# Attention scores in fp32r from stacked high and low key parts, in the mixers of the last two blocks

## The reference, cut to what matters

```python
def _diff_attention(dq, dk, dv, lam):
    s = jnp.einsum('bqhjd,bkhjd->bhjqk', dq, dk).astype(jnp.float32) * ATTN_SCALE
    p = jax.nn.softmax(s, axis=-1)
    a = (p[:, :, 0] - lam * p[:, :, 1]).astype(dv.dtype)
    return jnp.einsum('bhqk,bkhe->bqhe', a, dv)

def _gqa_attention(gq, gk, gv):
    s = jnp.einsum('bqhgd,bkhd->bhgqk', gq, gk).astype(jnp.float32) * ATTN_SCALE
    p = jax.nn.softmax(s, axis=-1).astype(gv.dtype)
    return jnp.einsum('bhgqk,bkhd->bqhgd', p, gv)
```

## Time and profile before

| | us |
|---|---|
| median of 3 runs | 4083.15 (4079.98 to 4084.63) |
| the profiled execution, its own time | 4075.62 |
| its span, first to last instruction | 4073.8 |
| TensorE busy | 3853.2 (95%) |
| VectorE busy | 2133.5 (52%) |
| ScalarE busy | 1346.3 (33%) |
| GpSimd busy | 1484.0 (36%) |

### The profile page before, as it was taken

One profiled execution on the slowest core, in us unless ns is written; L12 is line 12 of the kernel. 1 busy time (PEld: TensorE's weight loads), 2 busy tenths in 40 slices (PEclk: granted clock), 3 DMA queues, 4 the chain that ended last, 5 costly groups with the idle time before them and its releaser, 6 DMA issues.

```text
span 4073.8 us, 48594 instructions
## 1 busy us (share of the span) xinstructions
PE 3853.2 (95%) x18340; PEld 3096.0 (76%) x18340; DVE 2133.5 (52%) x2959; ACT 1346.3 (33%) x1779; POOL 1484.0 (36%) x1012
## 2 busy tenths in 40 slices
PE   8999898999998989999999899999798999999999
PEld 7888775877886848757888778888675757777887
DVE  5555846036776361457732357777644348624334
ACT  3222644242224242352232332222424252334223
POOL 3555341436663202103433224444221305544443
PEclk9999999999999999999999999999899999999999
DMA  5554221224442101101122123333110202222222
GB/s 216 185 188 174 75 94 39 103 81 154 157 155 85 56 1 52 47 1 49 66 73 73 52 104 124 124 124 124 48 52 21 78 1 83 93 103 75 95 98 83
DMA packets 57650, 367.28 MB, mean 90 GB/s; under 512 B 5792, under 2 KB 12192, under 8 KB 14112
## 3 DMA queue, kind: packets, MB, share of 16 engines
q1 hardware_dynamic: 42064, 271.11, 19.1%
q10 hardware_dynamic: 15440, 94.12, 6.2%
HBM read 363.11 MB, written 2.10 MB: 90 GB/s over the span
## 4 chain that ended last, share of the span: by engine, by line
issue 62%; POOL 28%; PE 9%; POOLq 0%; DVE 0%; ACT 0%; DVEq 0%; ACTq 0%
POOL b_wlo L602 28%; PE ps L1768 3%; PE ps L1770 3%; PE ps L1769 3%; POOLq L616 0%; DVE b_y L1260 0%; POOLq L618 0%; DVE b_x L1264 0%; DVE b_y L1317 0%; PE ps L1844 0%; ACT b_whi L643 0%; PE ps L1831 0%; ACT b_xout L709 0%; DVE b_small L1262 0%; POOLq L602 0%
## 5 line engine op out<-in xcount | busy, mean ns | idle before, releaser
L602 POOL TENSOR_TENSOR b_wlo<-b_raw,b_whi 128x512 fp32r<-128x512 f32 x1008 | 1483.8, 1504 | 2569.3 <-ACT b_whi L643 2569.3
L1768 PE MATMUL ps<-b_hhi,b_whi 128*128 128x512 f32 x3032 | 1118.4, 369 | 21.1 <-POOL b_wlo L602 12.8
L1769 PE MATMUL ps<-b_hlo,b_whi 128*128 128x512 f32 x3032 | 1108.9, 366 | 0.0
L1770 PE MATMUL ps<-b_hhi,b_wlo 128*128 128x512 f32 x3032 | 1108.3, 366 | 0.0
L643 ACT ACTIVATE b_whi<-b_raw 128x2048 fp32r<-128x2048 f32 x252 | 481.5, 1911 | 902.1 <-PE ps L1770 877.5
L1768 PEld LDWEIGHTS ps<-b_hhi,b_whi 128*128 128x128 f32 x3032 | 573.2, 189 | 126.1 <-issue 22.7
L1769 PEld LDWEIGHTS ps<-b_hlo,b_whi 128*128 128x128 f32 x3032 | 573.6, 189 | 93.3 <-issue 1.9
L1770 PEld LDWEIGHTS ps<-b_hhi,b_wlo 128*128 128x128 f32 x3032 | 573.0, 189 | 93.0
L1317 DVE TENSOR_TENSOR b_y<-ps,b_y 128x512 f32<-128x512 f32 x496 | 335.6, 689 | 242.0 <-PE ps L1770 242.0
L1768 PE MATMUL ps<-b_whi,b_dhi 128*128 128x512 f32 x992 | 393.6, 397 | 0.1
L1770 PE MATMUL ps<-b_whi,b_dlo 128*128 128x512 f32 x992 | 393.4, 397 | 0.0
(11 more groups left out here) (306 smaller groups left out, 4674.7 us busy)
## 6 DMA issues: line engine op xcount, KB each, us to landing
b_raw<-panels SPq DMA_DIRECT2D x252, 1024.0 KB, 4.7
b_mraw<-mod_panels ACTq DMA_DIRECT2D x78, 1024.0 KB, 4.9
b_y<-mod_panels ACTq DMA_DIRECT2D x3, 1024.0 KB, 15.8
b_xin<-xT SPq DMA_DIRECT2D x1, 2048.0 KB, 25.4
b_mraw<-mod_panels SPq DMA_DIRECT2D x2, 1024.0 KB, 17.1
b_crow<-par ACTq DMA_DIRECT2D x2, 1024.0 KB, 5.1
b_rope<-rope ACTq DMA_DIRECT2D x4, 512.0 KB, 3.5
outT<-b_xout SPq DMA_DIRECT2D x4, 512.0 KB, 3.6
```

What stands on the lines that cost most here:

```text
L602: ins = pool.tensor_tensor(wlo[:, s, c], raw[:, s, c], whi[:, s, c].bitcast(F32), ALU.subtract)
L1768: pe.matmul(out, a[0], b[0], start=first, stop=False)
L1769: pe.matmul(out, a[0], b[1], start=False, stop=False)
L1770: return pe.matmul(out, a[1], b[0], start=False, stop=last)
```

## The change

Scores are now two accumulating fp32r passes. With k = kh + kl and q = qh + ql (h the fp32r copy, l the remainder), a tile of 128 partitions holds kh in the 64 rows of a head and kl in the other 64. Pass one has qh in both halves (qh.kh + qh.kl), pass two ql in both halves (ql.kh + ql.kl). A 768-key step becomes four fp32r matmuls: 512 and 512, 256 and 256 columns.

- ScalarE writes the high parts: keys of d (`pair_keys_hi`, 4 tiles x 2 maps, 64x768 each), keys of g (`key_hi`, 2 x 64x768), and for every unit two copies of its queries, once into each half (`pair_hi` for each map of d, `query_hi` for g).
- VectorE writes the low parts (`pair_keys_lo`, `key_lo`, `pair_lo`, `query_lo`); the memsets of the padded tile and `masked_query` go.
- In d each map has one query tile: `pair_hi` waits until the last row of the unit before has been scored. In g the two tiles alternate.
- Heads of g are now projected gk first, gq 0 to 3, then gv; the values are turned inside attention g, behind its first two score steps.

```diff
+    def units_at(self, r, ahead):
+        return [n for n in range(1, len(self.units)) if max(self.first_row(n) - ahead, -1) == r]
...
+    query_split = lambda v: (qs0, qs1)[v % 2]
+    pair_split = lambda j: (qs0, qs1)[j]
+    own_rows = lambda half: slice(64 * half, 64 * half + 64)
...
+            def query_hi(rows, v):
...
+                act.wait_ge(*at(*rows.query_event(X, t, g)))
+                if v == 1:
+                    act.wait_ge(*at("roped", X("gq", 3)))
+                if v >= 2:
+                    act.wait_ge(*at("scores", X("g", rows.last_row(v - 2), rows.unit(v - 2)[1])))
+                act.activation(query_split(v)[o, 0, 0:b - a], aq[o, t, a:b], ACT.Copy, scale=SCALE).then_inc(*up("c_hi", X("q own", v)))
+                act.activation(query_split(v)[own_rows(1 - half), 0, 0:b - a], aq[o, t, a:b], ACT.Copy, scale=SCALE)\
+                   .then_inc(*up("c_hi", X("q", v)))
+
+            def pair_hi(rows, v, j):
...
+                if v == 0:
+                    act.wait_ge(*at("roped", X("dq", 3)))
+                else:
+                    act.wait_ge(*at("scores", X("d", rows.last_row(v - 1), j)))
+                o = own_rows(j)
+                act.activation(pair_split(j)[o, 0, 0:b - a], aq[o, t, a:b], ACT.Copy, scale=SCALE).then_inc(*up("c_hi", X("p own", v, j)))
+                act.activation(pair_split(j)[own_rows(1 - j), 0, 0:b - a], aq[o, t, a:b], ACT.Copy, scale=SCALE)\
+                   .then_inc(*up("c_hi", X("p", v, j)))
...
             def attention(rows):
                 for step in rows.first_steps():
                     row_exp(rows, *step)
+                if rows.tag == "g":
+                    keep_values()
+                    for v in rows.units_at(-1, 5):
+                        query_hi(rows, v)
                 for r in range(len(rows)):
...
                     for step in steps[1 if rows.tag == "d" else 0:]:
                         row_exp(rows, *step)
+                    if rows.tag == "d":
+                        for j in range(2):
+                            if r + 3 - j < len(rows) and rows.unit_start(r + 3 - j):
+                                pair_hi(rows, rows.unit_no(r + 3 - j), j)
+                    for v in rows.units_at(r, 5) if rows.tag == "g" else ():
+                        query_hi(rows, v)
                 keep_output(rows, len(rows) - 1)
...
                     act.activation(dk[:, 2 * a + n, L:TT], ps[:, 2 * (2 * a + n) % 4 + 1, 0:LC], ACT.Copy)\
                        .then_inc(*up("ctx_kept", X("dk", 2 * a + n)))
+                for n in range(2):
+                    pair_keys_hi(2 * a + n)
...
             rows = ROWS(st, "d")
+            for j in range(2):
+                pair_hi(rows, 0, j)
             attention(rows)
...
+            def pair_lo(rows, v, j):
...
+                dve.wait_ge(*at("c_hi", X("p", v, j)))
+                src, hi = aq[o, t, a:b], pair_split(j)[o, 0, 0:b - a].bitcast(F32)
+                dve.scalar_tensor_tensor(pair_split(j)[o, 1, 0:b - a], src, SCALE, hi, ALU.mult, ALU.subtract)
+                dve.scalar_tensor_tensor(pair_split(j)[own_rows(1 - j), 1, 0:b - a], src, SCALE, hi, ALU.mult, ALU.subtract)\
+                   .then_inc(*up("qm", X("d", v, j)))
...
                 for r in range(len(rows)):
                     steps = rows.next_steps(r)
-                    for q, j in steps:
+                    for q, j in steps if rows.tag == "d" else ():
                         if rows.unit_start(q):
-                            masked_query(rows, q, j)
+                            pair_lo(rows, rows.unit_no(q), j)
+                    for v in rows.units_at(r, 3) if rows.tag == "g" else ():
+                        query_lo(rows, v)
                     row_probs(rows, r)
...
+            def split_scores(rows, r, j):
...
+                for n, (c0, c1) in enumerate([(k0, L), (L, k1)] if k0 == 0 else [(k0, k1)]):
+                    for part in range(2):
+                        ins = pe.matmul(ps[:, b + n, 0:c1 - c0], q[:, part, :], keys[:, c0:c1], start=(part == 0), stop=(part == 1))
                 ins.then_inc(*up("scores", X(rows.tag, r, j)))
...
                 for step in rows.first_steps():
-                    row_scores(rows, *step, keys)
+                    scores(rows, *step)
+                if rows.tag == "g":
+                    turn_values()
```

More of the change, by code:

```diff
@@ L321, in bank, with first_row, last_row @@
         return 2 * (j if self.tag == "d" else r % 2)
+    def first_row(self, n):
+        return [row[0] for row in self.rows].index(n)
+    def last_row(self, n):
+        return max(r for r, row in enumerate(self.rows) if row[0] == n)
+    def units_at(self, r, ahead):
+        return [n for n in range(1, len(self.units)) if max(self.first_row(n) - ahead, -1) == r]
     def last_row_with(self, n, j):
@@ new lines, in pair_hi @@
+            def pair_hi(rows, v, j):
+                t, half, g = rows.unit(v)
+                a, b = GROUPS[g]
+                act.wait_ge(*at(*rows.query_event(X, t, g)))
+                if v == 0:
[6 more added lines that the diff above has]
+                   .then_inc(*up("c_hi", X("p", v, j)))
@@ L1583, in row_probs, with query_lo @@
                        .then_inc(*up("probs", X(rows.tag, r)))
-            def first_queries(rows):
-                for half in range(2):
-                    o = 64 * (1 - half)
-                    chain(dve.memset(qm2[o:o + 64, half, :], 0.0))
-                for r, j in rows.first_steps():
-                    if rows.unit_start(r):
-                        masked_query(rows, r, j)
+            def query_lo(rows, v):
+                t, half, g = rows.unit(v)
+                a, b = GROUPS[g]
+                o = own_rows(half)
+                dve.wait_ge(*at("c_hi", X("q", v)))
+                src, hi = aq[o, t, a:b], query_split(v)[o, 0, 0:b - a].bitcast(F32)
+                dve.scalar_tensor_tensor(query_split(v)[o, 1, 0:b - a], src, SCALE, hi, ALU.mult, ALU.subtract)
+                dve.scalar_tensor_tensor(query_split(v)[own_rows(1 - half), 1, 0:b - a], src, SCALE, hi, ALU.mult, ALU.subtract)\
+                   .then_inc(*up("qm", X("g", v, half)))
             def attention(rows):
@@ L2231, in weigh, with turn_values, attention @@
                 ins.then_inc(*up("pv", X(rows.tag, uno)))
-            def attention(rows, keys, values):
+            def turn_values():
+                pe.wait_ge(*at("v_kept", X()))
+                claim([4, 5], ("gv", X()))
+                for t in range(6):
+                    ins = pe.transpose(ps[:, 4 + t // 4, (t % 4) * P:(t % 4 + 1) * P], pr2[:, 0, 1, t * P:(t + 1) * P], const("ident"))
+                ins.then_inc(*up("v_turned", X()))
+            def attention(rows, scores, values):
                 for step in rows.first_steps():
-                    row_scores(rows, *step, keys)
+                    scores(rows, *step)
+                if rows.tag == "g":
+                    turn_values()
                 for r in range(len(rows)):
                     for step in rows.next_steps(r):
-                        row_scores(rows, *step, keys)
+                        scores(rows, *step)
                     if r >= 1 and rows.unit_end(r - 1):
```

183 lines of the change are left out of this document (102 added, 81 removed).

## The result

The changed kernel takes 4168.33 us (median of 4 runs, 4167.70 to 4171.84), the kernel before beside it 4081.57 (4 runs, 4078.36 to 4084.63): ratio 1.0222, 95% interval 1.0209 to 1.0234. It is slower by 86.8 us. The forecast was slower by 66.2, with 4172 as its upper end; by the ratio the change would put the 4083.15 us of the forecast at 4174. The direction and the mechanism came out, the size did not.

What follows compares the result with a forecast made beforehand. It took attention d as set by exp, probabilities and maximum, not TensorE, and g as nearly TensorE-bound. Terms of +44.7 at full clock and +21.5 for the clock gave +66.2 on 4083.15: 4149 us, range 4100 to 4172.

Steps and rivals of the forecast that it cites:

- the split delay: Mix3, d: four high key copies ahead of a panel split whose low part TensorE already awaits: +2.9 us.
- The clock's parts: TensorE's clock falls in sparse stretches: 11 us in d's products, 11 in g of mix2; together +21.5, bounds 0 and 35.
- The layout for mix3: Attention d, mix3: a unit timed from product end; query preparation stops VectorE, next product at 22.4 instead of 16.7, +5.7 us.
- +8.8 a pair, three times, +5.1 for the first: Attention d, mix2: late long-unit scores and VectorE's stops cost this per long and short pair; +32.7 us with start and tail.
- VectorE's ring: Attention d: exp (1.03), probabilities (1.85) and maximum (0.95 to 0.99) set each row, 3.85 us, not TensorE.
- so only the products cost: Attention d at low clock: slower scores and transposes stay hidden, 4 + 3 products take 1.55 us more each, 11 us.
- five cold products of eight: Attention g, mix2: five of eight pairs pay low clock at a transpose (+0.7) and a product (+1.55), 11 us.
- Eight units, about -14: Attention g, mix3: query preparation lies under the product; product end to next start falls from 8.93 to 7.1 us.
- Rival 1: Both attentions: VectorE's stops come as laid out but TensorE's clock holds; +45, 4128 us, chance 0.22.
- Rival 4: Clock stays low through both d attentions, products too, and all eight pairs of g in mix2; 4170 us, chance 0.06.
- Rival 2: TensorE sets the pace, query work is hidden, VectorE does not stop at pair_lo; 4004 at best, likely 4040, chance 0.09.
- Rival 3: Attention g gains more, -50, and d loses only minimal stops; within 10 us of 4083, chance 0.08.

Runs made afterwards that it cites:

- e1: Changed kernel with attention d's high query copies moved to just behind ScalarE's first exp, ahead of the row copy and second exp: 4123.15 us, ratio 1.0103.
- e2: Changed kernel with attention d's low query parts moved behind the probabilities of the row on VectorE: 4151.50 us, ratio 1.0175.
- e4: Changed kernel with attention d back to plain fp32 scores, masked queries and one full copy of each key tile; g stays split: 4089.17 us, ratio 1.0026.
- e9: Changed kernel with a third ScalarE copy of the same size added to each pair_hi, later overwritten: 4175.78 us, ratio 1.0237.
- e3: Changed kernel with six overwritten key products filling TensorE's gap ahead of each unit's first scores in attention d: 4159.93 us, ratio 1.0193.
- e5: Changed kernel with attention d's high key copies moved behind ScalarE's next panel split: 4170.92 us, ratio 1.0220.
- e6: Changed kernel with attention g's low query parts moved behind the probabilities of the same row: 4145.26 us, ratio 1.0162.
- e8: Changed kernel with attention d in plain fp32 scores (full key copies kept) and g's low query parts behind the probabilities: 4071.03 us, ratio 0.9980.
- e11: Changed kernel with attention d wholly as before, without key copies, and g split with low parts behind the probabilities: 4063.20 us, ratio 0.9964.

## Why the forecast was right and where it failed

The traces differ by 93.1 us where 66.2 were forecast. Of the 26.9 missing, 11.2 are in attention d of mix2, 5.7 in g of mix3 (a gain that did not come), about 2 in g of mix2, 1.7 in the split delay, 1.2 in d of mix3 and 4.5 in the rest. (The clock's parts, 7 x 1.55 and 5 x 2.25, add up to 22.1; the forecast's sum has 21.5.)

**Right: the place and the chain.** `pair_lo` stops VectorE for ScalarE's copies behind the exp. The layout for mix3 had the low parts start 7.0 us after the product's end and measured 7.2 (3152.37 - 3145.15); product end to next product start was put at 22.4 and came to 23.5 and 23.7, from 16.7. e1, e2 and e4 bear it out, and e9 prices a copy at its own length. The attention d of mix3 as a whole was put at 117 and came to 118.5, but that is luck in part: the 4.7 us put for three cold products did not come, and in their place the intervals between products were 1.1 and 1.3 us longer than laid out and the first product 2.2 us later. A fused subtract of 512 takes 0.68 to 0.69. The Trainium skill, "VectorE: DVE Perf Modes", section "The TRN2 errata — SBUF-src ops pay a fixed extra latency per instruction", has a formula for an fp32 tensor_tensor addition that gives 0.69 at 512 (an estimate for this operation; the forecast named the section on tiers for it); the trace agrees, and the bounds from other lengths (0.75) were 0.06 high.

**Failed: "+8.8 a pair, three times, +5.1 for the first", attention d of mix2.** This is the step that failed by most, 11.2 us. Product end to product start was 35.20 and 35.19 us (1456.08 to 1491.28, 1497.37 to 1532.56) instead of 31.6, then 30.7 for the last. The first product starts 37.5 us into the stage against 24.8 before, so +12.6 where 6.8 were put (5.1 and 1.7). Two things were sized too small or left out. The stage now begins with TensorE stopped 3.10 us for the first low parts, against 0.63 before (2.5 more, where 1.7 was put), and its clock is low from there (0.55 from the first score to the first product). In mix3, where the rows are simpler, the same start shows it:

```profile
3107.07 1.10 PE L2326 MATMUL ps<-b_kd,b_qs 128*128 128x512 f32 x4 [3.10 <-issue]
...
3110.43 1.62 PE L2326 MATMUL ps<-b_kd,b_qs 128*128 128x512 f32 x4 [0.33 <-ACT b_pr L985]
```

A step that takes 0.93 us of records at full clock takes 1.62 to 1.65 there, and each stands in the chain from exp to maximum. And behind every stop the next steps are slow too: windows of the same unit have 0.57 and 0.52 behind the two sets of stops and 1.00 between them.

```profile
1460.80:1466.70 5.90, 5.42 (x19) 4.38 (x20) 4.86 (x9) 2.26 (x5) 0.00 (x0) 0.57 0.00 0
1466.70:1475.60 8.90, 5.13 (x31) 3.93 (x29) 6.17 (x10) 6.14 (x13) 0.00 (x0) 1.00 0.00 0
1475.60:1491.30 15.70, 6.70 (x25) 5.32 (x26) 9.18 (x18) 5.95 (x14) 0.00 (x0) 0.52 0.00 0
```

The forecast said that "slower scores and transposes still fit beside VectorE's ring, so only the products cost". Here it is the first maximum behind a stop that waits for a slow score. Where the 3.6 us a pair arise can be read off the same pair, at the second map of its long unit, first the changed kernel (its product ended at 1456.08):

```profile
1460.82 2.93 PE L2326 MATMUL ps<-b_kd,b_qs 128*128 128x512 f32 x8 [4.36 <-DVE b_qs L1637]
...
1463.50 0.90 ACT L985 ACTIVATE b_pr<-ps,b_small 128x768 f32<-128x768 f32 x1 [4.16 <-DVE b_small L1656]
```

then the kernel before (its product ended at 1467.16):

```profile
1469.87 0.90 ACT L958 ACTIVATE b_pr<-ps,b_small 128x768 f32<-128x768 f32 x1 [0.75 <-DVE b_small L1568]
```

In the changed kernel the score starts 4.7 us behind the product's end, where 4.4 was put. The exp is late by 7.42 - 2.71 = 4.7, where 3.7 was put: the maximum starts 1.7 us behind the slow score's start, and behind one at full clock 1.0 (3145.73 to 3146.70). So 1.0 of the 3.6 are there already, 0.7 of them the clock. The other 2.6 fall behind this exp, where 5.1 were put for the two stops of the short unit and the first of the next long one, and 7.7 came. Between the two stops of the short unit the clock has no part in them. In the last pair of the changed kernel the first stop's score (at 1558.01) takes 0.80 us and the transposes behind it 1.54, and the second stop's score starts 6.78 us later; in e3 it is 0.51 and 0.87, and still 6.79 us (from 1554.23). The second stop's score, first of the changed kernel, then of e3:

```profile
1564.79 0.80 PE L2326 MATMUL ps<-b_kd_seven,b_qs 128*128 128x256 f32 x2 [3.28 <-DVE b_qs L1637]
```

```profile
1561.02 0.50 PE L2329 MATMUL ps<-b_kd_seven,b_qs 128*128 128x256 f32 x2 [1.27 <-DVE b_qs L1637]
```

From stop to stop it is the chain of probabilities, maxima, exp, row copy, exp, query copies and low parts on VectorE and ScalarE, and the layout had it too short. By how much at each step, the forecast does not say, since it gives only the sum of 5.1.

**Partly failed: "so only the products cost: 4 + 3 more, 11 us".** Mix2's four products cost 3.8 us more than before (24.9 against 21.2), mix3's first three none: 5.14, 5.15, 5.15. The score step just ahead of each ran at full clock already (0.93 at 3139.24), which in mix2 it did not.

**Right in sum, wrong in parts: g of mix2.** +17 was put, +19.3 came. I had five cold products of eight; it was seven, worth 8.5 us in all where products were put at 8. The stretches between the products, with the stop in the third row, cost 8.0, where 6 and 3.5 for the clock's transposes were put, and 2.8 more lie ahead of the first product, where nothing was put. The Trainium skill, "TensorE: Matmul & The Clock Gate", section "HAM oscillation", holds that an engine left idle pays at every return. The trace agrees here: all seven products behind a stop were cold, and the eighth has no stop. In mix3's attention d the rule came true for the scores right behind the stop (up to 1.65 us against 0.96), not for the products 7 us behind it, which were warm.

**Failed: "Eight units, about -14", g of mix3.** A gain was counted for each of eight units. There are seven intervals, and the last one was short before as well (12.65 us, nothing to prepare), so six gained: 14.15 to 12.54, that is 1.6 each and 9.7 in all. 0.5 in the last interval and 1 us at the two ends go against it: -8.3. The unit itself was right (product end to start 7.25, put at 7.1).

**Failed by size: the split delay.** 2.9 was taken, the four copies at 0.7; they take 0.84 each and the wait grew by 4.6. e5 shows that it is mostly their place (3.8 of it). For the rest GpSimd's low part takes longer; it runs beside VectorE's new key subtractions:

```profile
3049.72 13.44 POOL L629 TENSOR_TENSOR b_wlo<-b_raw,b_whi 128x512 fp32r<-128x512 f32 x8 [11.71 <-ACT b_whi L670]
...
3056.82 0.79 PE L1874 MATMUL ps<-b_hhi,b_whi 128*128 128x512 f32 x1 [4.99 <-POOL b_wlo L629]
```

TensorE goes on 7.10 us after its four quarters began; in the kernel before it was 5.98 (2974.39 to 2980.37).

**The rivals.** Rival 1 (the clock holds) is out by the granted clocks of attention d, 0.69 and 0.77. Rival 4 (4170, clock low through both d attentions) is nearest in time, by luck: it put what the forecast lacked on the clock, while mix3's products were warm and 5.7 us of the missing are g's gain in mix3, 1.7 the split delay and 4.5 the rest. Rival 2 needed the copies to be ready in time: e1 made most of them so, and d was still slower than before, since VectorE's extra work remained. Even the deciding place that I named would not have made the split a gain in d. Rival 3 had g gain 50 us; e6 turns g of mix2 from a loss of 19.3 into a gain of 1.6, and with that of mix3 the sum is about 13.

## What to carry to other kernels

Before matmuls are made cheaper, ask which engine sets the row. Where VectorE does, as in attention d, a split that puts 1.4 us of VectorE work a query tile in the place of 0.4, for 0.57 us less TensorE work a step, loses even in the best order found; where TensorE nearly does, as in g, it wins 11 us in one mixer once the preparation lies under a long product. Put an operand's preparation behind the work of its engine that others already wait for (probabilities before low parts: 23 us for two moved lines), and ahead of the work that only it waits for. Count gains by the intervals that have them, not by the units.

## What the runs showed of the hardware

TensorE's clock reacts to a single gap in an otherwise dense stage. In attention g of mix2 one gap of 3.1 us in each pair, with rows of work around it, took the clock of the window from 0.99 to 0.91, and the product that comes 1.8 to 2.6 us behind the gap from 5.25 to as much as 6.65 us. With the gap at 1.6 us (e6) no product was cold; in e8 and e11 one of the eight was (5.93 and 5.85 us). Filling gaps with products nobody needs does raise the clock (0.69 to 0.80) but bought only 3 us of a stage that had lost 50.

VectorE's subtraction for a half key tile (64 x 768, fp32r out) took 0.95 us nine times and 1.90 to 1.94 seven times (the 16 of attention d in the changed kernel). All seven slow ones run beside GpSimd's subtractions of a panel (3049.72 above); of the nine fast ones only one does, in part. GpSimd's take 1.68 us each there (13.44 for 8) against a mean of 1.51. Which of the two slows the other, or whether both do, no run here takes apart.
